# Seven block products in place of eight in the up-projections of two of the three feed-forward groups

## Chip, cores and metric

One NeuronCore of a Trainium2 chip runs the whole kernel. The metric is the device time of one launch in microseconds. The kernel before takes 2788.84 us (median of 3 runs, 2787.46 to 2789.62).

## What is computed

A two-layer network runs over 640 tokens: 512 latent tokens and 128 context tokens, 1024 channels each. Each layer is feed-forward, token mixing (attention and a Fourier branch), feed-forward, each with a modulation in front and a normalisation behind. The change touches only the two feed-forward sub-layers of each layer, so four in all:

```python
def _swiglu(u, w_up, w_down):            # w_up: 1024 x 5632, w_down: 2816 x 1024
    a, g = jnp.split(u @ w_up, 2, axis=-1)
    return (jax.nn.silu(g) * a) @ w_down
```

`a` is the value and `g` the gate. Everything is float32.

## The kernel before

**Layout.** Channels lie on the 128 partitions, tokens along the free dimension. The 1024 input channels are 8 blocks `k` of 128. The 640 tokens are 2 halves `h` of HT = 320. The 2816 hidden channels are 22 blocks, done in three groups of 8, 8 and 6 (`GROUPS`).

**Precision.** Each float32 operand is split in two parts of fewer bits, high and low: `Uh`/`Ul` for the modulated input, `w_hi`/`w_lo` for a weight, `Hh`/`Hl` for the hidden values. One block product is three matmuls into one accumulator: high by high, high by low, low by high.

**Weights.** They come as a stream of tiles of 16 blocks of 128x128 (1 MB). SP loads tile t into `w_raw[t % 2]` when the tile two before it has been split (`s_wsplit`). ACT rounds it to `w_hi` (`round_tile`, L922), DVE subtracts for `w_lo` (`low_tile`, L1240). Both are one tile ahead of TensorE. An up tile holds, for one hidden block, 8 blocks of the value and 8 of the gate.

**Up stage** (`ffn`, loops `up` on TensorE, ACT and DVE). For one tile TensorE does, for each token half, 8 block products into the value bank and 8 into the gate bank of one PSUM "use" (2 banks; four uses go round): 2 x 16 x 3 = 96 matmuls of 320 columns (L631, L633, L634). Then ACT takes silu of the gate bank into `sg` (`gate_half`, L1009), DVE multiplies with the value bank into `hf` (`product`, L1424), rounds to `Hh` (L1433) and subtracts for `Hl` (L1434). Every second tile DVE also works off two chunks of the conditioning weights (`ada_pair`, L1260 and L1262, four passes over 1024 columns), which ACT loads (`load_ada`).

**Down stage.** After each group four weight tiles (three after the group of 6) bring the hidden blocks back to 1024 channels (L444 to L447; `down_halves`, L489 to L493, after the last group), and DVE adds the result into `X`. The down stage starts on the first hidden blocks at once and waits for the last one block by block (`hidden_ready`).

**First group.** Its first 4 tiles (`EARLY`) are handled apart (`opening`, `first_up`), with the buffers `spare_f` and `spare_h`. The remaining 4 go through the loop `up`.

**POOL** does nothing but four constants at the start. `link` on DVE is a wait for DVE's own last instruction.

Of the kernel before, what the change touches and what calls it, by code (L numbers as in the profile page):

```python
# [13 lines left out]
P = 128  # L14
# [33 lines left out]
PIECES = 11  # L48
BIAS_STEP = {1: 0, 2: 1, 3: 2, 5: 3, 6: 4, 7: 5}
# [46 lines left out]
def build(nc, a):  # L96
    ctx = ExitStack()
    with ctx:
# [7 lines left out]
        X = sb("X", [P, KD, T])  # L106
        Uh = sb("Uh", [P, KD, T], F32R)
        Ul = sb("Ul", [P, KD, T], F32R)
        w_raw = sb("w_raw", [P, 2, 16, P])
# [42 lines left out]
        spare_f = spare("spare_f", 5120, 13312)  # L152
        spare_h = spare("spare_h", 61440, 81920)
# [132 lines left out]
        s_out = sem("y_stored")  # L286

# [11 lines left out]
        s_stands = {e: sem("wait_taken_" + e) for e in ("pe", "act", "dve")}  # L299
        block = ctx.enter_context(nc.Block())  # L300

        def make(which, **other):
# [6 lines left out]
                kv=s_kv, ada=s_adone, dve=s_dve, wraw=s_wload[0], whi=s_whi)  # L309
            first = dict(use=4, tile=1, ada=1, u=2 * KD, u32=2 * KD, mrg=4) | other  # L310
# [63 lines left out]
        def _(pe):  # L374

            C = make("tile use full h u mean sum sqsum var att sc max exp pt ptc o of fill fev mix mrg".split(), u=0)
# [236 lines left out]

            def ffn(pending):
# [4 lines left out]
                for group, size in enumerate(GROUPS):  # L619
# [17 lines left out]
                    pairs(size // 2 - (EARLY // 2 if group == 0 else 0), 2, 4, up)  # L637
# [264 lines left out]
        def _(act):  # L902
            C = make("use full func mods u32 u xc sq added var std xn y att max exp pt ptc o mrg ada kv wraw whi".split())
# [19 lines left out]

            def down_tiles(with_ada):
                def trip(i):
                    round_tile()
                    if with_ada:
                        ada_pair()
                    round_tile()
                over(act, 2, [(C["wraw"], 16), (C["whi"], 2)] + [(C["ada"], 2)] * with_ada, trip, act_met)  # L930
# [4 lines left out]
            def ada_pair():  # L935


                for s in (1, 0):
                    c = C["ada"].at()
                    if not isinstance(c, int):  # L940
                        c = act.snap(c)
                    act.wait_ge(s_adone, c)
                    load_ada(c + FIRST_ADA, s)
                    C["ada"].next()
# [39 lines left out]
            def last_products(l, s, spares, more):  # L984

                round_tile()
                for i, spare in enumerate(spares):
                    round_tile(1 + i, spare)
# [90 lines left out]
            def ffn(l, s):  # L1079
# [4 lines left out]
                for group, size in enumerate(GROUPS):  # L1084
                    def up(i):
                        for e in range(4):
# [3 lines left out]
                            if e == 0:  # L1090
                                ada_pair()

                    start = use_no[0]
                    n = size // 2 - (EARLY // 2 if group == 0 else 0)
                    over(act, n, [(use, 4), (C["full"], 4), (C["func"], 4), (C["ada"], 2), (C["wraw"], 16),
                                  (C["whi"], 2)], up, act_met)
                    use_no[0] = start + 4 * n
# [125 lines left out]
        def _(dve):  # L1223
            C = make("use full func h mods u32 u mean sum sq sqsum added std xc xn att kv max sc exp of fill fev pt o mix mrg ada dve whi".split())
# [5 lines left out]
            def low_tile(spare=None):  # L1230
# [9 lines left out]
                dve.tensor_tensor(lo, w_raw[:, r, :, :], hi.bitcast(F32), ALU.subtract).then_inc(s_wsplit, 1)  # L1240

# [152 lines left out]
            def down(m, n_of, count, ada):  # L1394

                for n in range(count):
                    if n % 2 == 0:
                        low_tile()
# [13 lines left out]
            def down_loop(m, ada=None):  # L1412
                start = use_no[0]
                over(dve, 2, [(use, 4), (C["full"], 4), (C["whi"], 2)]
                     + ([(C["ada"], 2), (C["dve"], 3)] if ada else []),
                     lambda i: down(m, lambda n: i * 4 + n, 4, (lambda: ada(i)) if ada else None), dve_met)
                use_no[0] = start + KD
# [482 lines left out]
```

## Time and profile before

| | |
|---|---|
| median of 3 runs | 2788.84 us |
| the profiled execution, device time | 2792.42 us |
| its span, first to last instruction | 2790.6 us |
| TensorE busy in the span | 2731.4 us (98%) |
| DVE, ACT, POOL busy | 60%, 27%, 0% |
| mean granted TensorE clock | 0.993 of full |

Matmuls are pipelined: a row's duration is the time through the array, and the rate is seen from start to start. On DVE an instruction without a wait starts some 0.08 us before the one ahead of it ends, so there too the spacing counts.

### The profile page before, as it was taken

To read this page: it belongs to the slowest core of one execution; us is meant where nothing else is said; L and a number is where in the kernel's file an instruction comes from. 1 tells how busy PE (TensorE), PEld (TensorE's weight loads), DVE (VectorE), ACT (ScalarE), POOL (GpSimd) and SP (SyncE) were. 2 spreads that over 40 slices of the span, in tenths; PEclk is the share of its full clock that TensorE was granted. 3 is DMA by queue.
4 is the path that set the end of the run, shared out by engine and by line. 5 is a ranking of instruction groups with operands and counts; after the bars stand their busy time and mean duration, and the time that the engine had idled before them with its cause. 6 is when DMAs were issued, how large, how long until landed. Compare 5 with 4: busy or idle time off the path is not lost.

```text
span 2790.6 us, 47327 instructions
## 1 busy us (share of the span) xinstructions
PE 2731.4 (98%) x18772; PEld 2702.6 (97%) x18772; DVE 1664.6 (60%) x3108; ACT 751.4 (27%) x1082; POOL 0.2 (0%) x4
## 2 busy tenths in 40 slices
PE   8999999899999999999999999998999999999997
PEld 8999999899999999999999999998999999999996
DVE  6645465765765864445686454676476568445456
ACT  4111112533221611111252111234242234111113
POOL 0000000000000000000000000000000000000000
PEclk9999999999999999999999999999999999999998
DMA  7434332211333132323223333322213322223231
GB/s 280 141 119 132 112 128 91 87 66 59 106 121 121 61 136 89 107 91 121 76 99 129 105 120 113 128 76 72 78 62 121 135 89 99 99 98 113 85 127 38
DMA packets 77781, 295.15 MB, mean 106 GB/s; under 512 B 25168, under 2 KB 31568, under 8 KB 54096
## 3 DMA queue, kind: packets, MB, share of 16 engines
q1 hardware_dynamic: 51552, 211.16, 21.8%
q10 hardware_dynamic: 26096, 82.16, 8.8%
q8 instruction: 91, 1.49, 0.2%
q14 instruction: 42, 0.34, 0.0%
HBM read 289.62 MB, written 6.82 MB: 106 GB/s over the span
## 4 chain that ended last, share of the span: by engine, by line
PE 92%; DVE 5%; DMA 1%; ACT 1%; issue 0%; ACTq 0%; SPq 0%; DVEq 0%
PE psum L633 12%; PE psum L634 12%; PE psum L631 12%; PE psum L446 6%; PE psum L444 6%; PE psum L447 6%; PE psum L489 3%; PE psum L492 3%; PE psum L493 3%; PE psum L858 3%; PE psum L860 3%; PE psum L861 3%; PE psum L693 2%; PE psum L876 1%; PE psum L874 1%; PE psum L877 1%
## 5 line engine op out<-in xcount | busy, mean ns | idle before, releaser
L631 PE MATMUL psum<-Uh,w_hi 128*128 128x320 f32 x2304 | 712.0, 309 | 0.0
L633 PE MATMUL psum<-Ul,w_hi 128*128 128x320 f32 x2304 | 711.9, 309 | 0.0
L634 PE MATMUL psum<-Uh,w_lo 128*128 128x320 f32 x2304 | 711.9, 309 | 0.0
L922 ACT ACTIVATE w_hi<-w_raw 128x2048 fp32r<-128x2048 f32 x166 | 317.6, 1913 | 590.5 <-PE psum L444 317.2
L631 PEld LDWEIGHTS psum<-Uh,w_hi 128*128 128x128 f32 x2304 | 432.5, 188 | 0.2 <-issue 0.2
L633 PEld LDWEIGHTS psum<-Ul,w_hi 128*128 128x128 f32 x2304 | 432.5, 188 | 0.0
L634 PEld LDWEIGHTS psum<-Uh,w_lo 128*128 128x128 f32 x2304 | 432.5, 188 | 0.0
L1240 DVE TENSOR_TENSOR w_lo<-w_raw,w_hi 128x2048 fp32r<-128x2048 f32 x166 | 380.3, 2291 | 81.1 <-ACT w_hi L922 76.7
L1424 DVE TENSOR_TENSOR hf<-sg,psum 128x320 f32<-128x320 f32 x176 | 85.7, 487 | 409.5 <-ACT sg L1009 407.6
L447 PE MATMUL psum<-Hh,w_lo 128*128 128x320 f32 x1024 | 316.2, 309 | 0.0
L444 PE MATMUL psum<-Hh,w_hi 128*128 128x320 f32 x1024 | 316.2, 309 | 0.0
L446 PE MATMUL psum<-Hl,w_hi 128*128 128x320 f32 x1024 | 316.2, 309 | 0.0
L1009 ACT ACTIVATE sg<-psum 128x320 f32<-128x320 f32 x176 | 77.0, 437 | 866.6 <-PE psum L634 614.8
L1408 DVE SCALAR_TENSOR_TENSOR X<-psum,mods,X 128x320 f32 (+2 forms) x192 | 72.6, 434 | 237.0 <-PE psum L447 237.0
L1260 DVE CUSTOM_DVE_ANT_0 junk<-ada_w,csilu 128x1024 bf16<-128x1024 f32 x144 | 176.0, 1222 | 62.8 <-DVEq L1724 48.4
L447 PEld LDWEIGHTS psum<-Hh,w_lo 128*128 128x128 f32 x1024 | 192.5, 188 | 0.0
L444 PEld LDWEIGHTS psum<-Hh,w_hi 128*128 128x128 f32 x1024 | 192.5, 188 | 0.0
L446 PEld LDWEIGHTS psum<-Hl,w_hi 128*128 128x128 f32 x1024 | 192.5, 188 | 0.0
L1262 DVE CUSTOM_DVE_ANT_0 junk<-ada_w,csilu 128x1024 bf16<-128x1024 f32 x144 | 176.4, 1225 | 5.0
L858 PE MATMUL psum<-Uh,w_hi 128*128 128x320 f32 x512 | 158.4, 309 | 0.9 <-DVE Ol L1651 0.9
L860 PE MATMUL psum<-Ul,w_hi 128*128 128x320 f32 x512 | 158.2, 309 | 0.0
L861 PE MATMUL psum<-Uh,w_lo 128*128 128x320 f32 x512 | 158.2, 309 | 0.0
(236 smaller groups left out, 4903.0 us busy)
## 6 DMA issues: line engine op xcount, KB each, us to landing
w_raw<-in_wstream SPq DMA_DIRECT2D x184, 1024.0 KB, 4.9
ada_w<-in_ada ACTq DMA_DIRECT2D x145, 512.0 KB, 3.7
first_w<-in_ada SPq DMA_DIRECT2D x9, 512.0 KB, 14.3
first_w<-in_ada_first SPq DMA_DIRECT2D x6, 512.0 KB, 9.1
gath<-in_rpb SPq DMA_DIRECT2D x128, 24.0 KB, 3.4
G<-gath ACTq DMA_DIRECT2D x4, 768.0 KB, 4.5
X<-in_xT SPq DMA_DIRECT2D x8, 320.0 KB, 15.1
yT<-X SPq DMA_DIRECT2D x16, 160.0 KB, 1.8
```

Source lines behind the costliest of these rows:

```text
L444: m1 = pe.matmul(out, wh, rh, start=(k == 0), stop=False)
L446: pe.matmul(out, wh, rl, start=False, stop=False)
L447: mm = pe.matmul(out, wl, rh, start=False, stop=(k == nk - 1))
L631: m1 = pe.matmul(out, wh, rh, start=(k == 0), stop=False)
L633: pe.matmul(out, wh, rl, start=False, stop=False)
L634: mm = pe.matmul(out, wl, rh, start=False, stop=(k == KD - 1))
L858: m1 = pe.matmul(out, wh, rh, start=(k == 0), stop=False)
L860: pe.matmul(out, wh, rl, start=False, stop=False)
L861: mm = pe.matmul(out, wl, rh, start=False, stop=(k == KD - 1))
L922: act.activation(hi, w_raw[:, r, :, :], ACT.Copy).then_inc(s_whi, 1)
L1240: dve.tensor_tensor(lo, w_raw[:, r, :, :], hi.bitcast(F32), ALU.subtract).then_inc(s_wsplit, 1)
L1262: i = dve.tensor_tensor_reduce(junk[:, :], ada_w[:, s, :], csilu[:, 1, :], 1.0, 0.0, ALU.mult, ALU.add, acc4[:, 1, s:s + 1])
```

## The change

In groups 2 and 3 of each feed-forward sub-layer (8 + 6 = 14 tiles, four times, 56 tiles) an up tile is taken as a 2x2 block matrix: value and gate by the two halves of the input channels (4 blocks each). The input is a 2x2 block matrix too: two halves of the input channels by two token halves. The 2x2 product is made from seven block products (Winograd's form of Strassen's scheme) instead of eight. Each product is 4 blocks deep, 4 x 3 = 12 matmuls of 320 columns.

- **Operands of the weights**: parts 0, 1 and 3 and four sums. POOL makes the sums, 4 instructions of 512 columns per tile (`weight_sums`), into columns of `Uh` and `Ul` that no product reads. ACT rounds and DVE splits each of the 7 operands by itself, 512 columns each (`round_operand`, `low_operand`), into a ring in `w_hi`/`w_lo`. Operand j of the next tile takes the place of operand j of this one, after product j.
- **Operands of the tokens**: four sums for each of 4 block rows, made once per sub-layer by POOL (`token_sums`, 4 x 10 instructions of 320 columns) during the loop tiles of the first group. ACT rounds and DVE splits them into `Th`/`Tl`.
- **Products**: three accumulators x, y, z in PSUM. ACT copies them out while they grow (`copy_product`, four copies of 320 columns per tile into `snaps`). DVE makes the two value halves by two additions (`hf`), POOL adds the late gate (`late_gate`), ACT takes silu of `snaps[3]` and of x.
- **Hidden values** (`hidden_half`): `Hh` and `hf` are both products with `sg`, the latter in place, and `Hl` their difference; the cast is gone.
- The loading of conditioning chunks is spread over two tiles (`ada_chunk`). The loops of the first group and of the down stage on ACT and DVE are written out.
- After the last group ACT waits until the last use is free before it writes `spare_f`, whose place `snaps` and `Th` share.

```diff
+OPERANDS = (("part", 0), ("sum", 0), ("sum", 1), ("part", 1), ("sum", 2), ("sum", 3), ("part", 3))
...
+            def seven_products(i):                                    # TensorE
...
+                U = (Uh, Ul)
+                for _ in range(2):
+                    u, v = next_use(), next_use()
+                    x, y, z = bank(u, 0, 0, HT), bank(u, 1, 0, HT), bank(v, 0, 0, HT)
+                    order = ((x, moving(U, 0, 0), True, 0), (y, summed(0), True, 0), (x, summed(1), False, 1),
+                             (z, moving(U, 4, 0), True, 0), (x, summed(2), False, 3), (y, moving(U, 4, 1), False, 2),
+                             (x, summed(3), False, 4))
+                    for j, (out, mv, start, copied) in enumerate(order):
+                        if copied:
+                            pe.wait_ge(s_snap, C["snap"].at(-copied))
+                        if j < 6:
+                            pe.wait_ge(s_opsplit, C["opsplit"].next())
...
+                        for k in range(4):
...
+                        mm.then_inc(s_prod, 1)
...
+            def seven_products(prepare, s):                           # ACT
...
+                product_done()
+                act.wait_ge(s_add, C["add"].at(1))
+                copy_product(0, x)
+                prepare(0)
+                product_done()
+                copy_product(1, y)
+                prepare(1)
+                product_done()
+                act.wait_ge(s_add, C["add"].at())
+                copy_product(2, x)
+                prepare(2)
+                product_done()
+                prepare(3)
+                product_done()
+                act.wait_ge(s_func, C["func"].at())
+                copy_product(3, x)
+                prepare(4)
...
+                product_done()
+                prepare(5)
+                act.wait_ge(s_late, C["late"].next())
+                act.wait_ge(s_free, use.at())
+                act.activation(sg[:, 1, :], snaps[:, 3, :], ACT.Silu).then_inc(s_func, 1)
...
+                product_done()
+                act.activation(sg[:, 0, :], x, ACT.Silu).then_inc(s_func, 1)
...
+                prepare(6)
...
+            def seven_products(at, prepare, between=None):            # DVE
...
+                for j in range(4):
+                    prepare(j)
...
+                mark(dve.tensor_tensor(hf[:, 0, :], snaps[:, 0, :], z, ALU.add), "add")
+                if between is not None:
+                    between()
+                for j in range(4, 6):
+                    prepare(j)
...
+                mark(dve.tensor_tensor(hf[:, 1, :], snaps[:, 2, :], y, ALU.add), "add")
+                dve.wait_ge(s_add, C["add"].at())
+                hidden_half(at, 1)
+                hidden_half(at, 0)
+                prepare(6)
...
+            def weight_sums(r):                                       # POOL
...
+                n1 = step(pool.tensor_tensor(part_sum(0), part(r, 2), part(r, 3), ALU.add), "wsum")
+                pool.wait_ge(s_wsum, n1)
+                n2 = step(pool.tensor_tensor(part_sum(1), part_sum(0), part(r, 0), ALU.subtract), "wsum")
+                step(pool.tensor_tensor(part_sum(2), part(r, 0), part(r, 2), ALU.subtract), "wsum")
+                pool.wait_ge(s_wsum, n2)
+                step(pool.tensor_tensor(part_sum(3), part(r, 1), part_sum(1), ALU.subtract), "wsum")
...
+                def trip(i):
+                    weight_sums(r ^ 1)
+                    late_gate()
+                    weight_sums(r)
+                    late_gate()
```

## Rows read from the trace of the kernel before

**Rows 1.** The page: busy time and share of each engine, then the slices.

```profile
PE 2731.4 (98%) x18772; PEld 2702.6 (97%) x18772; DVE 1664.6 (60%) x3108; ACT 751.4 (27%) x1082; POOL 0.2 (0%) x4
...
PE   8999999899999999999999999998999999999997
...
DVE  6645465765765864445686454676476568445456
```

**Rows 2.** Windows: first sub-layer's loop tiles of group 1, groups 2 and 3.

```profile
core 0: us, PE busy (x) PEld busy (x) DVE busy (x) ACT busy (x) POOL busy (x), PEclk, DMA share, GB/s
...
89.50:146.00 56.50, 56.50 (x385) 56.25 (x384) 38.61 (x62) 10.95 (x12) 0.00 (x0) 1.00 0.46 144
...
202.40:315.20 112.80, 112.80 (x771) 112.80 (x770) 59.13 (x92) 21.38 (x23) 0.00 (x0) 1.00 0.37 120
...
371.40:455.80 84.40, 84.40 (x578) 84.40 (x577) 49.14 (x78) 15.98 (x17) 0.00 (x0) 1.00 0.34 118
```

**Rows 3.** Groups by line, TensorE, and one line's own view (duration min/median/max).

```profile
L633 PE MATMUL psum<-Ul,w_hi 128*128 128x320 f32 x2304 | 711.9, 309 | 0.0
...
L631 PE MATMUL psum<-Uh,w_hi x2304: 307/309/408, 89.6 to 2723.7; 128*128 128x320 f32 x192
```

**Rows 4.** Timeline of ACT in group 2: start us, us, instruction, idle before it.

```profile
216.84 0.44 ACT L1009 ACTIVATE sg<-psum 128x320 f32<-128x320 f32 x1 [6.60 <-DVE acc L1262]
...
223.88 0.44 ACT L1009 ACTIVATE sg<-psum 128x320 f32<-128x320 f32 x1 [4.79 <-PE psum L634]
230.92 0.44 ACT L1009 ACTIVATE sg<-psum 128x320 f32<-128x320 f32 x1 [6.60 <-PE psum L634]
```

**Rows 5.** Waits over the whole run: us in total, times, longest.

```profile
ACT sg L1009 <- PE psum L634: 614.8, 119, 6.7
DVE hf L1424 <- ACT sg L1009: 407.6, 139, 5.7
...
PE psum L462 <- DVE sqtotal L1339: 12.5, 4, 6.6
```

**Rows 6.** Timeline of DVE in group 2 and group 3, with a conditioning pair.

```profile
210.27 0.49 DVE L1424 TENSOR_TENSOR hf<-sg,psum 128x320 f32<-128x320 f32 x1 [3.20 <-ACT sg L1009]
210.91 0.33 DVE L1433 CAST Hh<-hf 128x320 f32 x1
211.36 0.49 DVE L1434 TENSOR_TENSOR Hl<-hf,Hh 128x320 f32 x1
211.77 1.22 DVE L1260 CUSTOM_DVE_ANT_0 junk<-ada_w,csilu 128x1024 bf16<-128x1024 f32 x1
...
217.31 0.49 DVE L1424 TENSOR_TENSOR hf<-sg,psum 128x320 f32<-128x320 f32 x1 [0.19 <-ACT sg L1009]
...
378.56 2.29 DVE L1240 TENSOR_TENSOR w_lo<-w_raw,w_hi 128x2048 fp32r<-128x2048 f32 x1 [0.33 <-DVE mods L1267]
380.77 0.48 DVE L1424 TENSOR_TENSOR hf<-sg,psum 128x320 f32<-128x320 f32 x1
```

**Rows 7.** Groups by line and shape, DVE and ACT: busy us, mean ns.

```profile
L1240 DVE TENSOR_TENSOR w_lo<-w_raw,w_hi 128x2048 fp32r<-128x2048 f32 x166 | 380.3, 2291 | 81.1 <-ACT w_hi L922 76.7 <-DVE mods L1267 2.2 <-DVE mods L1275 1.3
...
L1434 DVE TENSOR_TENSOR Hl<-hf,Hh 128x320 f32 x144 | 71.0, 493 | 18.3 <-DVE Hh L1433 0.9
...
L1354 DVE RECIPROCAL std<-std 128x320 f32<-128x320 f32 x12 | 25.8, 2153 | 15.5 <-ACT std L957 15.5
```

```profile
L922 ACT ACTIVATE w_hi<-w_raw 128x2048 fp32r<-128x2048 f32 x166 | 317.6, 1913 | 590.5 <-PE psum L444 317.2 <-DVE acc L1262 84.4 <-PE psum L858 74.0
...
L1046 ACT ACTIVATE Uh<-u 128x320 fp32r<-128x320 f32 x16 | 7.5, 471 | 0.5
```

**Rows 8.** Groups by line, POOL: one of its four rows, all alike.

```profile
L1896 POOL MEMSET const-bfloat16-1.0<- 128x1 bf16 x1 | 0.1, 102 | 0.0
```

**Rows 9.** Timeline of DVE at the last group's end, in the last sub-layer.

```profile
2724.86 0.49 DVE L1424 TENSOR_TENSOR hf<-sg,psum 128x320 f32<-128x320 f32 x1 [5.45 <-ACT sg L1009]
...
2725.93 0.49 DVE L1434 TENSOR_TENSOR Hl<-hf,Hh 128x320 f32 x1
```

**Rows 10.** DMA issues: KB each, us from issue to landing.

```profile
w_raw<-in_wstream SPq DMA_DIRECT2D x184, 1024.0 KB, 4.9
```

More of the change, by code:

```diff
@@ L374, in _ @@
         def _(pe):
-            C = make("tile use full h u mean sum sqsum var att sc max exp pt ptc o of fill fev mix mrg".split(), u=0)
+            C = make("tile use full h u mean sum sqsum var att sc max exp pt ptc o of fill fev mix mrg opsplit prod snap tlow".split(), u=0)
             tile, use = C["tile"], C["use"]
@@ L635, in up @@
                                 filled(mm)
-                    pairs(size // 2 - (EARLY // 2 if group == 0 else 0), 2, 4, up)
+                    if group == 0:
+                        pairs((size - EARLY) // 2, 2, 4, up)
+                    else:
+                        if group == 1:
+                            pe.wait_ge(s_tlow, C["tlow"].next(4))
+                        start = use_no[0]
+                        over(pe, size // 2, [(tile, 2), (use, 4), (C["prod"], 14), (C["opsplit"], 12), (C["snap"], 8)],
+                             seven_products, pe_met)
+                        use_no[0] = start + 2 * size
                     made = C["h"].at()
@@ L902, in _ @@
         def _(act):
-            C = make("use full func mods u32 u xc sq added var std xn y att max exp pt ptc o mrg ada kv wraw whi".split())
+            C = make("use full func mods u32 u xc sq added var std xn y att max exp pt ptc o mrg ada kv wraw whi wsum prod snap late add tsum".split())
             use = C["use"]
@@ L924, in down_tiles, with round_token_sums @@
+            def round_token_sums(k):
+                act.wait_ge(s_tsum, C["tsum"].next(10))
+                act.activation(Th[:, :, k, :], snaps[:, :, :], ACT.Copy).then_inc(s_thi, 1)
             def down_tiles(with_ada):
-                def trip(i):
+                for i in range(2):
                     round_tile()
@@ L986, in last_products @@
                 round_tile()
+                act.wait_ge(s_free, use.at())
                 for i, spare in enumerate(spares):
@@ L1091, in up @@
                                 ada_pair()
[L1093 to L1097, printed above, removed]
+                            if e % 2 == 1:
+                                round_token_sums(2 * i + e // 2)
+                    if group == 0:
+                        for i in range((size - EARLY) // 2):
+                            up(i)
+                    else:
+                        seven_run(size)
                     if group < 2:
@@ L1412, in down_loop @@
             def down_loop(m, ada=None):
[L1413 to L1417, printed above, removed]
+                for i in range(2):
+                    down(m, lambda n: i * 4 + n, 4, (lambda: ada(i)) if ada else None,
+                         (low_tile, low_tile if i == 0 else first_operands))
             def product():
@@ L1557, in up @@
                             for h in range(2):
-                                evacuate(bass.ds(i * 2 + (m + done), 1), h)
+                                evacuate(i * 2 + (m + done), h)
                                 if (m, h) == (0, 0):
                                     more_chunks(i)
-                    start = use_no[0]
-                    n = (size - done) // 2
-                    over(dve, n, [(use, 4), (C["full"], 4), (C["func"], 4), (C["h"], 4), (C["ada"], 2),
-                                  (C["dve"], 4 + 3), (C["whi"], 2)], up, dve_met)
-                    use_no[0] = start + 4 * n
+                            split_token_sums(2 * i + m)
+                    if group == 0:
+                        for i in range((size - done) // 2):
+                            up(i)
+                    else:
+                        seven_run(size, more_chunks)
                     chunk += size - done
```

256 lines of the change are left out of this document (240 added, 16 removed).

## The prediction

> **What bounds the kernel now.** I read the page's busy line first [rows 1]: TensorE is busy 98% of the span, DVE 60%, ACT 27%, POOL 0%. The slices say that this holds from end to end. The windows [rows 2] narrow it to the stages that change: in groups 2 and 3 TensorE has no idle time at all, at a full granted clock (2.4 GHz), while DVE works 59.1 of 112.8 us and ACT 21.4. The waits agree [rows 5]: ACT waits for TensorE (614.8 us) and DVE for ACT (407.6 us), and the longest total wait of TensorE is 12.5 us, at a normalisation. So in these stages time is the number of matmuls times their spacing. The duration of 309 ns [rows 3] isn't the spacing. It is seen from the gates [rows 4]: one comes every 7.04 us (216.84, 223.88, 230.92), and between two of them are 48 matmuls, so 0.1467 us each. A tile of 96 takes 14.08 us, and 112.8 us hold 8 of them.
>
> **What is removed.** A tile goes from 96 matmuls to 7 x 12 = 84, same shape. That is 12 x 0.1467 = 1.76 us less per tile, which then takes 12.32 us. With 56 tiles: 98.6 us. Each product lasts 1.76 us, and everything below has to be measured against that, not against 3.7 us, which the durations would suggest.
>
> **TensorE's new waits.** At each product it now waits for an operand and often for a copy of its accumulator. The present loop has waits and a branch at each use boundary, and the spacing of 7.04 us shows no cost. The worst L631 is 0.1 us over the median [rows 3]; at each of 392 product boundaries that would be 39 us. I take 0 and keep 39 as the other end. A copy has one product (1.76 us) to be made: 0.44 us [rows 4] plus some 0.3 us of latency. It fits, if ACT is at hand.
>
> **ACT.** From 1913 ns for 2048 columns and 471 for 320 [rows 7], 512 columns cost 0.63 us. Per tile: 7 x 0.63 + 4 copies x 0.44 + 2 silus x 0.45 = 7.1 us of 12.32. It fits. ACT is in order though: behind its wait for the late gate (POOL) and for sums (POOL) stand the copies that TensorE waits for.
>
> **DVE.** From 2291 ns for 2048 columns and 493 for 320 [rows 7], 512 columns cost 0.69 us, or 0.61 from start to start, since a following instruction starts 0.08 us early (378.56 to 380.77 is 2.21 us for one of 2.29 [rows 6]). A linked one of 320 columns takes 0.63 to 0.64 from start to start, an unlinked one 0.41 (210.27, 210.91, 211.36, 211.77 [rows 6]). A conditioning pair takes 5.5 us (211.77 to 217.31). For two tiles:
> 14 low parts x 0.61 = 8.5; 4 additions, half of them linked, 2.1; hidden halves 4 x (0.63 + 0.63 + 0.41) = 6.7; one pair 5.5. The sum is 22.8 us of 24.64, or 93%.
> DVE goes from idle to nearly full. The order has to be gone through as well. Product 3 of a tile ends 7.04 us into it, ACT's rounding makes it 7.9, and DVE has low part 3 done at 8.5. In a tile with a pair there follow the addition (8.9), the pair (14.4), low parts 4 and 5 (15.6), the second addition (16.2), both hidden halves (19.6) and low part 6 (20.2). TensorE needs those three at 19.4, 21.1 and 22.9. The next tile catches up, since it has no pair: its hidden halves end at about 28.3, and low part 3 is again ready 8.5 us into the tile after. So TensorE isn't held. If instead each low part takes its full 0.69 us and a wait of 0.15 us (what a link adds), two tiles take 26.0 us, 0.7 us per tile too much: 39 us. I take 0, since operands lie ready when DVE comes to them.
>
> **POOL.** No row has arithmetic on POOL; its rows are four constants [rows 8]. Call p the time of its sum of 512 columns. From below p = 0.69 us, DVE's own price. From above I take the slowest elementwise row, the reciprocal of 320 columns in 2153 ns [rows 7]: 6.7 ns a column, p = 3.4. A simple addition is nearer to the first: I take 1.5 times DVE's price, p = 1.04, and 0.74 for 320 columns. A tile has four sums and a late gate, 4.9 us of 12.32. They may start when low part 5 is split (3.3 us into a tile without a pair) and when the raw tile has landed; its slot is free at about 3 us of the tile before, and landing takes 4.9 us [rows 10]. ACT wants the first sum at 4 us of that tile. It comes at 4.5, and the copy behind it is needed only at 7.04. It fits up to p of about 2. The Trainium skill ("GPSIMD Engine Reference", section 3.1) gives 4497 ns for 2048 columns of such an addition; an estimate from that page is 1.1 us for 512, and by it the sum below doesn't change. No run here shows it yet.
>
> **Token sums.** 40 POOL instructions x 0.74 = 30 us per sub-layer lie beside the 56 us of the first group's loop tiles. ACT gets 4 x 1.3 us and DVE 4 x 1.4 us more there, where DVE is busy 38.6 of 56.5 us [rows 2]. TensorE needs the result one down stage (56 us) later. Cost 0.
>
> **Starts of the down stage.** Now the last hidden block is ready about 1.6 us after its gate (2724.86 to 2726.42 [rows 9]); then 0.63 + 0.63 + 0.49 = 1.75 us. TensorE's cover there is 5 blocks x 3 x 0.147 = 2.2 us in group 3, about used up already. I count 0.3 us x 4 = 1.2 us. In group 2 the cover is three times as long. The weights' first operands of a group are made in the down stage, in the time of the tile that they replace, and operands 4 to 6 have four products' time. ACT's new wait for the last use stands ahead of a buffer needed some 28 us later: 0.
>
> **Sum.** The profiled execution took 2792.4 us. 2792.4 - 98.6 + 1.2 = 2695.0. It lay 3.6 us above the median, so I forecast 2691.4, say 2692 us.
>
> **Rivals.**
> (A) Forecast: TensorE stays the bound, 2686 to 2705.
> (B) DVE or the new waits show through. DVE has 7% left, and the two ends above are 39 us each. The price of one is 2692 + 39 = 2731; the case holds 2705 to 2783. Part-way contention with POOL falls here too. For it speaks that each tile with a pair already runs 1.8 us late and only the next one repairs it.
> (C) DVE and POOL exclude each other. Nearly all new DVE work reads two operands in SBUF, and so does POOL. If such instructions can't run at the same time, two tiles need the sum of both. DVE's are 14 x 0.69 + 12 x 0.49 + 4 x 1.22 = 20.4 us; POOL's are 8p + 2 x 0.71p = 9.4p. TensorE is held once 20.4 + 9.4p exceeds 24.64 (p over 0.45, so at any p within the bounds), and the kernel is slower than before once it exceeds 28.16: p over 0.82 us. At p = 1.04 it is 30.2 us, 1.0 us per tile more than before: 2789 + 57 = 2846. At p = 0.69 it is 2754. Nothing in the trace speaks for or against it, because POOL never works beside DVE; if it is so, the 40% that DVE is idle is no room for POOL.
> The Trainium skill ("SBUF — State Buffer", section "Who interferes with whom") states it: a DVE instruction with two SBUF inputs and a GpSimd instruction that reads SBUF contend for one read port, and the second to issue is blocked until the first ends. With that page's rule and the other page's 1.1 us the estimate would be 2869. No row here shows the pair of them.
> (D) POOL itself is too slow. At p = 3.4 a tile needs 4 x 3.4 + 2.2 = 15.8 us on POOL, 1.7 more than before: 2789 + 97 = 2886. It begins to cost at p over 2 and is slower than before from p of about 3.1.
> (E) The scheme doesn't shorten TensorE, for instance because accumulating again into a bank costs time. The counts in the code are plain: 84 matmuls of an unchanged shape.
>
> **How the numbers follow.** A 0.42, B 0.16, C 0.34, D 0.06, E 0.02. In C p below 0.82 leaves it faster, which takes 0.03 of its chance, and some 0.03 lie within 0.2%. Faster by over 0.2% is then 0.59, within it 0.04, slower 0.37; 0.2% (5.6 us) is about what a measurement of this kernel can tell from no change. The range must take in C: it runs from 2686 to 2875, which leaves out the slow end of C and most of D, some 0.14. A's own range is 2686 to 2705. It is wide because faster and slower cases both are likely.
>
> **What would show it.** Under A: TensorE without idle time in the windows of groups 2 and 3, 12.3 us from tile to tile, DVE above 90% busy there with low parts near 0.69 us, POOL's sums near 1.04 us. Under B: the same durations, but TensorE waiting for low parts or copies. Under C: durations of DVE or POOL that grow where both are active (low parts well over 0.69 us, conditioning passes over 1.22 us), 15 us per tile and TensorE idle, perhaps with a clock below full after it. Under D: sums of over 2 us with DVE's durations unchanged, ACT waiting for POOL. I'm wrong in the working if DVE's durations are unchanged and the time is still above 2735.

## The result and the profile after

The changed kernel takes 2863.82 us (median of 4 runs, 2862.61 to 2865.26) beside 2789.23 us for the kernel before on the same chip: a ratio of 1.027, 95% interval 1.025 to 1.0285. It is slower by 75 us where the forecast was 2692. Its profiled execution took 2865.26 us, with a span of 2863.4. Of the rivals it is C, the exclusion of DVE and POOL, that fits, though not by its own figures. Three steps of the sum failed with it (POOL's fit, the start of group 3, the token sums), one of them in a place where POOL isn't involved.

The page of the changed kernel first: busy time and count of each engine, then the slices of the span.

```profile
PE 2688.3 (94%) x18100; PEld 2640.2 (92%) x18100; DVE 2116.7 (74%) x3572; ACT 980.7 (34%) x1658; POOL 603.1 (21%) x444
...
PE   8999998899999999898999989898999999998996
...
DVE  7769778855765885968887796986476578679497
...
POOL 0534232000000062413106340400000002533130
```

Against [rows 1] TensorE has 672 matmuls fewer (56 tiles x 12), and its busy time fell by only 43 us, not by 98.6. DVE went from 60% to 74%, and POOL has 603 us of work where it had none. Seven slices of TensorE fell from 9 to 8, and POOL works in six of them.

Windows of the changed kernel, by stage, in the first sub-layer: loop tiles of the first group up to the down stage, down stage, group 2, group 3. Columns as in [rows 2].

```profile
88.20:152.80 64.60, 59.52 (x386) 58.74 (x384) 54.03 (x63) 14.63 (x16) 46.17 (x32) 0.95 0.35 107
152.80:209.30 56.50, 56.46 (x385) 56.46 (x386) 33.47 (x56) 9.11 (x8) 15.34 (x13) 1.00 0.40 126
209.30:326.50 117.20, 104.85 (x674) 102.77 (x673) 111.31 (x149) 51.59 (x101) 50.30 (x36) 0.96 0.35 111
...
382.90:474.80 91.90, 79.84 (x507) 77.78 (x505) 86.23 (x119) 38.69 (x75) 36.52 (x26) 0.94 0.29 99
```

| stage, us | before | after | times |
|---|---|---|---|
| first group's loop tiles | 56.6, later 56.3 | 64.6, later 59.2 | 1 and 3 |
| group 2 | 112.6 | 117.1 to 117.3 | 4 |
| group 3 | 84.5 | 91.6 to 91.9 | 4 |
| down stages of the first group | 56.3 | 56.4, 56.4, 58.0, 59.2 | 4 |
| first 162 matmuls of the last down stage, to the next one's start | 32.8 | 34.2 | 4 |

The times run from the first matmul of a stage to the first of the next. Groups 2 and 3 lose about 4 x (4.5 + 7.3) = 47 us, the first groups 8.0 + 3 x 2.9 = 17, the down stages of the first group 5 and the last ones 6: 75 in all. Against the forecast, which wanted 12.32 us a tile (4 x 172.5 = 690 us for groups 2 and 3), the 4 x (117.2 + 91.9) = 836 us are 146 too many.

In group 2 DVE is busy 111.3 of 117.2 us (95%, against 59.1 of 112.8 in [rows 2]). TensorE is idle 12.4 us of it and busy 104.9, though 672 matmuls at 0.1467 us are 98.6: the other 6 us are matmuls at the lower clock, which the granted clock of 0.96 shows.

Waits of the changed kernel over the whole run (total us, times, longest):

```profile
PE psum L682 <- ACT snaps L1040: 53.3, 28, 3.9
PE psum L682 <- DVE w_lo L1446: 41.3, 31, 2.3
...
ACT w_hi L1025 <- POOL sums L2082: 81.3, 39, 4.8
...
ACT Th L1107 <- POOL snaps L2060: 99.0, 13, 10.7
```

TensorE now waits for copies (L1040) and low parts (L1446), where the longest total of [rows 5] was 12.5 us. ACT waits for POOL's sums. That these stand behind both is seen in e2 below: with the sums cut short, 15.5 of the 94.6 us are left.

### The profile page after: what moved, and what is told of

Read it like the earlier page. It is cut to its first block and busy times, and to the rows that moved or that the text cites. A ratio compares the mean times of both kernels' runs of the same rounds, so it can differ in the third digit from the quotient of the medians.

```text
span 2863.4 us, 48177 instructions
## 1 busy us (share of the span) xinstructions
PE 2688.3 (94%) x18100; PEld 2640.2 (92%) x18100; DVE 2116.7 (74%) x3572; ACT 980.7 (34%) x1658; POOL 603.1 (21%) x444
## 5 line engine op out<-in xcount | busy, mean ns | idle before, releaser
L682 PE MATMUL psum<-Th,w_hi 128*128 128x320 f32 x896 | 292.9, 327 | 94.9 <-ACT snaps L1040 53.3
L1433 DVE TENSOR_TENSOR w_lo<-w_raw,w_hi 128x2048 fp32r<-128x2048 f32 x110 | 263.5, 2396 | 73.5 <-ACT w_hi L1009 72.9
L687 PE MATMUL psum<-Th,w_lo 128*128 128x320 f32 x896 | 286.7, 320 | 0.0
L686 PE MATMUL psum<-Tl,w_hi 128*128 128x320 f32 x896 | 286.4, 320 | 0.0
L682 PEld LDWEIGHTS psum<-Th,w_hi 128*128 128x128 f32 x896 | 175.5, 196 | 111.1 <-DVE w_lo L1446 66.1
L2082 POOL TENSOR_TENSOR sums<-w_raw 128x512 f32<-128x512 f32 x56 | 79.3, 1415 | 724.4 <-DVE w_lo L1446 411.0
L1025 ACT ACTIVATE w_hi<-sums 128x512 fp32r<-128x512 f32 x224 | 139.0, 627 | 248.5 <-POOL sums L2082 81.3
L682 PE MATMUL psum<-Uh,w_hi 128*128 128x320 f32 x672 | 211.9, 315 | 0.0
L686 PE MATMUL psum<-Ul,w_hi 128*128 128x320 f32 x672 | 210.7, 313 | 0.0
L687 PE MATMUL psum<-Uh,w_lo 128*128 128x320 f32 x672 | 209.6, 312 | 0.0
L687 PEld LDWEIGHTS psum<-Th,w_lo 128*128 128x128 f32 x896 | 177.2, 198 | 0.0
```

Source lines behind the costliest of these rows:

```text
L682: m1 = pe.matmul(out, hi[:, k, :], rh, start=(start and k == 0), stop=False, skip_group_check=not start)
L686: pe.matmul(out, hi[:, k, :], rl, start=False, stop=False, skip_group_check=not start)
L687: mm = pe.matmul(out, lo[:, k, :], rh, start=False, stop=(k == 3), skip_group_check=not start)
L1025: act.activation(two_rows(operand(w_hi, j, w_slot[0])), operand_source(op_raw[0], j), ACT.Copy)\
```

## Why DVE and POOL don't run side by side

Timeline of DVE in group 2 of the changed kernel (start us, duration, instruction, idle before it in brackets), and of POOL in the same stretch:

```profile
239.76 0.49 DVE L1658 TENSOR_TENSOR Hh<-sg,hf 128x320 f32 x1 [0.27 <-DVE hf L1685]
240.29 1.47 DVE L1659 TENSOR_TENSOR hf<-sg,hf 128x320 f32<-128x320 f32 x1
241.88 1.38 DVE L1667 TENSOR_TENSOR Hl<-hf,Hh 128x320 f32 x1
243.18 1.58 DVE L1658 TENSOR_TENSOR Hh<-sg,hf 128x320 f32 x1
```

```profile
240.11 1.29 POOL L2082 TENSOR_TENSOR sums<-w_raw 128x512 f32<-128x512 f32 x1 [6.59 <-DMA w_raw<-in_wstream]
241.48 1.43 POOL L2084 TENSOR_TENSOR sums<-sums,w_raw 128x512 f32<-128x512 f32 x1
242.87 1.54 POOL L2085 TENSOR_TENSOR sums<-w_raw 128x512 f32<-128x512 f32 x1
```

The first DVE instruction has no POOL beside it until its last 0.14 us and takes 0.49 us, as [rows 7] have it. The next starts at 240.29, while POOL's first sum is under way (240.11 to 241.40), and ends at 241.76, 0.36 us after that sum: alone it takes 0.49, so it can have done little before. POOL's next sum then outlasts it in turn. The two take turns, and each duration holds the wait for the other. One instruction of each together takes 1.50 us (the next two of DVE end at 243.26 and 244.76). The groups by line show DVE's products of 320 columns at nearly twice their 493 ns:

```profile
L1659 DVE TENSOR_TENSOR hf<-sg,hf 128x320 f32<-128x320 f32 x112 | 107.3, 958 | 7.8
...
L2082 POOL TENSOR_TENSOR sums<-w_raw 128x512 f32<-128x512 f32 x56 | 79.3, 1415 | 724.4 <-DVE w_lo L1446 411.0 <-DMA w_raw<-in_wstream 259.3 <-issue 54.0
```

The shortest instance of L2082 is 1.26 us: that is POOL's own price for 512 columns. How a sum that comes late reaches TensorE is seen in a tile with a conditioning pair. Four rows of the timeline, from POOL, ACT (two) and TensorE:

```profile
257.74 1.26 POOL L2082 TENSOR_TENSOR sums<-w_raw 128x512 f32<-128x512 f32 x1 [8.31 <-DVE w_lo L1446]
...
259.04 0.63 ACT L1025 ACTIVATE w_hi<-sums 128x512 fp32r<-128x512 f32 x1 [4.04 <-POOL sums L2082]
259.57 0.42 ACT L1040 ACTIVATE snaps<-psum 128x320 f32<-128x320 f32 x1
...
260.12 0.41 PE L682 MATMUL psum<-Th,w_hi 128*128 128x320 f32 x1 [2.08 <-ACT snaps L1040]
```

DVE had the pair to do and split low part 5 late, POOL may not write its sums before that, ACT stands at the rounding of the first sum, and the copy that TensorE needs is the next instruction in ACT's queue. TensorE loses 2.08 us, though the product that the copy reads had ended at 256.3.

## The experiments

Each edit is against the changed kernel unless it says otherwise. "Before" is the kernel before, run beside it.

**e2: POOL's four sums and the late gate of 8 columns.** Products read raw parts in place of the sums.

```diff
-n1 = step(pool.tensor_tensor(part_sum(0), part(r, 2), part(r, 3), ALU.add), "wsum")
+n1 = step(pool.tensor_tensor(short(part_sum(0)), short(part(r, 2)), short(part(r, 3)), ALU.add), "wsum")
```

> The changed kernel, but POOL's four weight sums and its late gate are cut to 8 columns each (same instructions, same waits, same order); ACT and DVE take the raw parts where they took the sums, so the up-projections of groups 2 and 3 are not those of the reference. DVE's, ACT's and TensorE's work is unchanged. Theory L (DVE and POOL exclude each other while both read SBUF): with POOL's reads gone the seven-product stages are bound by TensorE at 12.3 us per tile, DVE's low parts and hidden multiplies are back at 0.68 and 0.49 us; 98.6 us less than the kernel before, plus about 20 us still lost in the first groups, where POOL still makes the token sums: about 2712 us. Theory F (DVE is simply too full, or TensorE's new waits cost time, POOL's work is harmless): DVE has as much to do as in the changed kernel, so the time stays between 2840 and 2865 us.

Measured: 2740.34 us, ratio to before 0.982 (0.9806 to 0.9839). That is 123 us less than the changed kernel, with every instruction still issued. Group by line and windows (group 2; group 3 and 0.9 us of the stage behind it) of e2:

```profile
L1662 DVE TENSOR_TENSOR hf<-sg,hf 128x320 f32<-128x320 f32 x112 | 55.2, 493 | 7.7
```

```profile
209.30:307.80 98.50, 98.50 (x675) 98.50 (x673) 82.67 (x151) 50.62 (x100) 15.47 (x36) 1.00 0.42 137
...
364.10:444.60 80.50, 76.61 (x513) 76.35 (x512) 67.52 (x122) 38.51 (x76) 12.35 (x26) 0.98 0.37 124
```

DVE's product is back at 493 ns, and group 2 runs at exactly the 12.3 us a tile of the forecast, TensorE without idle time. Counts, waits and copies are those of the changed kernel, so TensorE's new waits cost nothing, as forecast. What is lost in group 2 comes from POOL's full-width sums; whether it is their reading beside DVE or only the time that they take is told apart by e5 and e8. But group 3 still takes 79.5 to 80.6 us, not 73.9, and that was expected by neither theory. TensorE and ACT at its start in e2:

```profile
368.33 1.67 ACT L1028 ACTIVATE w_hi<-w_raw 128x512 fp32r<-128x512 f32 x3 [15.75 <-DVE acc L1482]
371.12 0.44 ACT L1043 ACTIVATE snaps<-psum 128x320 f32<-128x320 f32 x1 [1.12 <-DVE acc L1482]
371.68 0.41 PE L685 MATMUL psum<-Th,w_hi 128*128 128x320 f32 x1 [3.89 <-ACT snaps L1043]
```

ACT waits 15.75 us for DVE's passes of a conditioning pair (`acc`), which stands between the last down tile and group 3, then again for its last pass, 1.12 us ahead of the copy. TensorE stands 3.89 us.

**e7: e2 with that extra pair ahead of the last down use.**

```diff
-                    if group == 1:
-                        chunks(chunk)(0)
-                        chunk += 2
+                        down_loop(mods[s], chunks(chunk) if s == 0 else None,
+                                  [lambda: chunks(extra)(0)] if group == 1 else ())
```

> The run with POOL's weight sums and late gate cut to 8 columns (raw parts taken as operands, so groups 2 and 3 are not the reference's), and one thing more: the conditioning pair that DVE works off between the last down product and the first low parts of group 3 now runs before DVE takes the last down use. Theory S (the start of group 3): in that run ACT stood 15.8 us in its wait for that pair, so operands 4 to 6 and the first copy came late, TensorE idled 3.9 us at product 2 and then ran at half clock; without it group 3 takes 6 x 12.3 us as it should, 5 to 7 us less in each of four sub-layers: about 2717 us. Rival: the first copy is late for another reason (ACT's order alone), and the time stays at 2740 us.

Measured: 2711.94 us, ratio 0.9725 (0.971 to 0.974), 28.4 us less than e2, 7.1 per sub-layer. Group 2 stays at 98.5 us; the window of group 3:

```profile
364.40:438.30 73.90, 73.90 (x507) 73.90 (x505) 61.54 (x112) 37.75 (x74) 11.49 (x26) 1.00 0.37 124
```

Both groups are now as forecast: 4 x (98.5 + 73.9) = 690 us. What e7 is above 2692, 20 us, lies elsewhere: 17 us of it in the first groups, beside the token sums.

**e3: the sums and the late gate on DVE, full width.** DVE gets four sums of 512 columns and one addition of 320 more per tile.

```diff
+                n1 = step(dve.tensor_tensor(part_sum(0), part(r, 2), part(r, 3), ALU.add))
...
+                mark(dve.tensor_tensor(snaps[:, 3, :], snaps[:, 3, :], snaps[:, 1, :], ALU.add), "late")
```

> The changed kernel with POOL's four weight sums and the late gate done by DVE, same values, same places; POOL keeps only the token sums. DVE, already the fuller engine, gets 8 x 0.60 + 2 x 0.41 us and two waits more for two tiles, some 6.4 us. Theory L: the sum for two tiles is then 22.8 + 6.4 = 29.2 us on DVE alone, 14.6 us per tile against 14.9 with POOL, and 14.08 in the kernel before; with 20 us lost in the first groups: about 2835 us, that is FASTER than the changed kernel although its busiest helper got more work. Theory F: 3.2 us per tile more than the changed kernel's 14.9: about 3040 us.

Measured: 2843.85 us, ratio 1.0196 (1.018 to 1.021), 20 us less than the changed kernel though DVE, the fuller engine, has all of POOL's weight sums and late gates. Without an exclusion I had expected 3040. Groups by line, and the window of the first group 2, of e3:

```profile
L1678 DVE TENSOR_TENSOR hf<-sg,hf 128x320 f32<-128x320 f32 x112 | 55.1, 492 | 8.3 <-DVE Hh L1677 0.7
```

```profile
210.60:326.70 116.10, 105.63 (x674) 104.85 (x673) 102.64 (x186) 49.78 (x99) 0.00 (x0) 0.93 0.36 113
```

POOL is still, DVE's durations are clean, and the four groups 2 take 116.1, 112.8, 112.8 and 116.1 us, where they took 117 with POOL's help. 186 DVE instructions do what DVE's 149 and POOL's 36 did.

**e5: conditioning passes of groups 2 and 3 cut from 1024 to 16 columns** (POOL as in the changed kernel).

```diff
-                    more_chunks = chunks(chunk)
+                    more_chunks = chunks(chunk, 16 if group else D)
```

> The changed kernel, with the conditioning passes of DVE in groups 2 and 3 cut from 1024 to 16 columns (14 x 4 passes per sub-layer; those modulation values are then wrong). DVE loses 4.6 us for two tiles. POOL is as it was. Theory L: what two tiles need from DVE's two-input instructions and POOL together is 15.5 + 11.8 = 27.3 us, 13.7 us per tile, still above TensorE's 12.3: about 2789 - 24 + 20 = 2785 us, and DVE's multiplies stay well over 0.49 us. Theory F: DVE has 17.5 us of work for 24.64 us of TensorE and is out of the way: about 2712 us.

Measured: 2766.54 us, ratio 0.992 (0.990 to 0.994), between the two expectations and nearer to that of the exclusion. Group 2 and the product's group by line:

```profile
209.30:312.70 103.40, 99.65 (x675) 98.60 (x674) 95.44 (x150) 51.47 (x100) 51.37 (x36) 1.00 0.41 130
```

```profile
L1659 DVE TENSOR_TENSOR hf<-sg,hf 128x320 f32<-128x320 f32 x112 | 108.3, 967 | 7.8
```

The product still takes 967 ns: POOL is in its way as before. What is gone is DVE's own work (28 passes per sub-layer; my expectation had counted 56), and the tile goes from 14.65 to 12.9 us. So POOL's sums at their full length, with all that waits for them, nearly fit once DVE has less to do. The sum by spacings for two tiles, 8.4 + 4.9 + POOL's 11.8 = 25.1 (worked out below), stands against 25.8 measured. I had expected 27.3, having counted durations where spacings hold.

**e4: the kernel before, with POOL working on data of its own** in layer 0: 74 additions from the start of group 2, 90 memsets in group 3, 74 copies in group 2 of the second feed-forward sub-layer. Apart from waits of ACT and DVE for the end of POOL's stretches, nothing else of the kernel changes.

```diff
+phase(14, 74, lambda o: pool.tensor_tensor(o, csilu[:, 0, 0:512], csilu[:, 1, 0:512], ALU.add))
+phase(26, 90, lambda o: pool.memset(o, 0.0))
+phase(TILES - 33 + 14, 74, lambda o: pool.tensor_copy(o, csilu[:, 0, 0:512]))
```

> The kernel before, with POOL working beside it on data of its own that nobody waits for, in layer 0: 74 additions of 512 columns with two SBUF inputs during group 2 of the first sub-layer, 90 memsets of 512 columns (it writes, reads nothing) during group 3, 74 copies of 512 columns (one input) during group 2 of the second feed-forward sub-layer. Theory L: in the first stretch DVE's instructions with two SBUF inputs (low parts 2.29 us, conditioning passes 1.22, Hl 0.49) take up to one POOL addition (about 1.3 us) longer, and POOL's additions take up to one DVE instruction longer, while the multiply that reads PSUM and one SBUF input stays at 0.49; with memsets nothing gets longer; with copies it is as with additions but shorter. The cast (one input, 0.33 us) shows which interface matters. TensorE has the slack, so the time stays within 0.3% of 2789 us. Theory F: no DVE duration changes in any stretch.

Measured: 2824.25 us, ratio 1.013 (1.011 to 1.014); the time was to be within 0.3%. DVE's groups by line and shape in group 2 of e4, with POOL adding all the while:

```profile
L1246 DVE TENSOR_TENSOR w_lo<-w_raw,w_hi 128x2048 fp32r<-128x2048 f32 x8 | 26.6, 3319 | 0.7 <-ACT w_hi L926 0.7
...
L1442 DVE TENSOR_TENSOR Hl<-hf,Hh 128x320 f32 x15 | 20.7, 1383 | 1.8
...
L1266 DVE CUSTOM_DVE_ANT_0 junk<-ada_w,csilu 128x1024 bf16<-128x1024 f32 x8 | 18.1, 2258 | 0.1
L1441 DVE CAST Hh<-hf 128x320 f32 x15 | 11.1, 738 | 2.2 <-DVE hf L1432 0.7
...
L1432 DVE TENSOR_TENSOR hf<-sg,psum 128x320 f32<-128x320 f32 x15 | 7.2, 480 | 3.1 <-ACT sg L1015 2.6
```

```profile
202.50:315.00 112.50, 112.50 (x770) 112.50 (x769) 103.78 (x89) 21.30 (x25) 112.50 (x61) 1.00 0.35 115
```

This is the disputed cost by itself. Against [rows 6, 7] every DVE instruction with two SBUF inputs grows by 0.9 to 1.0 us, most of one POOL addition (1.29): 2.29 to 3.32 us, 0.49 to 1.38, 1.22 to 2.26. The cast grows too (0.33 to 0.74). The product that takes one input from PSUM stays at 0.48. Beside POOL's copies, in the third stretch, it was the same in small: 2.29 to 2.63, 1.22 to 1.57, 0.49 to 0.69, the PSUM product at 0.49. TensorE loses nothing here: DVE's 103.8 us still fit into 112.5, which is why a kernel with a DVE 60% busy could hide it.

The 34.5 us came from the stretch with memsets (group 3: 117.6 us for 84.5). DVE's timeline in group 3 of e4, and what TensorE waited for:

```profile
372.51 1.23 DVE L1268 CUSTOM_DVE_ANT_0 junk<-ada_w,csilu 128x1024 bf16<-128x1024 f32 x1
...
376.31 35.95 DVE L1273 COPY mods<-acc 128x4 f32<-128x4 f32 x1
```

```profile
PE psum L635 <- DVE w_lo L1246: 31.1, 1, 31.1
```

Beside memsets the two-input pass is unchanged (1.23 us), but a copy of 4 columns stood 36 us.

**e10: memsets back to back in group 2, then with a gap after each in group 3** (e4's kernel).

```diff
+            phase(14, 60, lambda o: pool.memset(o, 0.0), 3)
+            phase(26, 60, lambda o: pool.memset(o, 0.0), 0)
```

> The kernel before with POOL on data of its own, in layer 0: 60 memsets of 512 columns back to back (up to four under way) in group 2 of the first sub-layer; 60 memsets of which each waits for the one before it, in group 3; 60 copies, each waiting for the one before, in group 2 of the second feed-forward sub-layer. Theory W (a DVE instruction of a mode that needs the shared interface for its writes is held until POOL lets go, and POOL's overlapping memsets never let go, as the small copy of 35.95 us in the first probe suggests): in the first stretch DVE's first cast or small copy hangs until the memsets are over, some 28 us, and TensorE may idle; in the second the memsets' gaps let it in, and casts and copies are longer by at most one memset (0.6 us), while instructions with two SBUF inputs stay at 2.29, 1.22 and 0.49 us in both. Rival: the 35.95 us had nothing to do with the memsets and no cast or copy takes more than 1 us.

Measured once: 2795.68 us. DVE's and POOL's timeline in group 2 of e10:

```profile
209.65 1.50 DVE L1441 CAST Hh<-hf 128x320 f32 x1
...
216.87 12.78 DVE L1273 COPY mods<-acc 128x4 f32 x1
```

```profile
201.68 27.95 POOL L1788 MEMSET probe<- 128x512 f32 x60 [201.22 <-PE psum L635]
```

The copy ended when the memsets did (229.6 us). The cast had come through after 1.50 us, where I had expected it to stand to the end. With gaps, casts took 0.33 to 0.56 us and no copy over 0.61. So memsets without a gap can keep a cast or copy of DVE from starting, but not each time; what decides it is open.

**e8: POOL keeps the sums; all conditioning pairs of groups 2 and 3 are made in the down stages.**

```diff
+            def down_loop(m, pairs):
+                places = (1, 2, 3) if len(pairs) == 6 else (1, 3)
...
-                    seven_products(bass.ds(i * 2, 1), low_operand, lambda: more_chunks(i))
+                    seven_products(bass.ds(i * 2, 1), low_operand)
```

> The changed kernel with POOL's sums as they are, and all conditioning pairs of groups 2 and 3 moved into the two down stages ahead of them (6 pairs in each in the first sub-layer of a layer, 4 in each in the last); values as in the reference. Theory L: the seven-product stages then have what the run with short conditioning passes had, two tiles needing 27 us less what overlaps; that run took 2766.5 us, and with the start of group 3 mended some 20 us less: about 2747 us, still above 2717 because DVE and POOL exclude each other. If the down stages get too full for DVE (about 50 of 56 us in the first sub-layer of a layer), TensorE waits there and it is 2760 to 2780 us. Theory F (no exclusion): TensorE-bound, 2715 us.

Measured: 2740.15 us, ratio 0.982 (0.981 to 0.984). Windows of group 2, down stage and group 3 in the first sub-layer, and of group 2 in the second feed-forward sub-layer:

```profile
209.50:316.60 107.10, 102.27 (x674) 101.22 (x674) 98.38 (x129) 51.05 (x100) 51.76 (x36) 0.97 0.32 101
316.60:372.90 56.30, 56.30 (x386) 56.30 (x385) 51.02 (x84) 8.56 (x9) 7.05 (x4) 1.00 0.53 178
372.90:448.90 76.00, 74.61 (x505) 73.83 (x505) 68.07 (x89) 37.59 (x73) 38.44 (x26) 1.00 0.26 90
...
1099.30:1200.50 101.20, 99.33 (x674) 98.54 (x674) 93.23 (x114) 51.06 (x100) 51.48 (x36) 1.00 0.24 83
```

The down stage takes six pairs and stays full on TensorE, its DVE at 51.0 of 56.3 us. In the second feed-forward sub-layer of each layer, with four pairs, group 2 takes 101.2 and 100.8 us, 25.2 per two tiles: what the sum by spacings gives without the pair (25.1), and near the 24.64 of TensorE. POOL's weight sums last 1.4 to 1.7 us in the mean, no less than in the changed kernel (1.4 to 1.6). So it isn't their length alone that makes 117 us there, but their length beside a DVE that is full. In the first sub-layer of each layer the sixth pair runs into group 2, which takes 107.1 us.

**e6: e8 with sums and late gate on DVE, and the cast back in the hidden halves.**

```diff
-                link(dve.tensor_tensor(hh, sg[:, h, :], hf[:, h, :], ALU.mult))
+                link(dve.tensor_copy(hh, hf[:, h, :]))
```

> A version meant to beat both kernels: weight sums and late gate on DVE (POOL only makes the token sums), all conditioning pairs of groups 2 and 3 moved into the down stages, and the hidden halves with a cast again (one product in place, then a cast of 0.33 us, then the difference), which POOL can't hold up any more. DVE for two tiles: 22 x 0.60 + 0.4 + 2.1 + 0.8 + 4 x (0.63 + 0.45 + 0.41) = 22.5 us of 24.64. Theory L: bound by TensorE, 2789 - 98.6 + about 20 us lost in the first groups to the token sums: 2710 us, 2700 to 2725. Rival: DVE at 91% of its time plus waits in ACT's and DVE's fixed order hold TensorE up by 0.5 us per tile or more, with half clock behind it: 2740 to 2780 us.

Measured (median of 5 runs): 2726.37 us, ratio 0.977 (0.976 to 0.9785), just above my range of 2700 to 2725 and, with e9, the fastest version that computes everything. Group 2 of the first and of the second feed-forward sub-layer:

```profile
209.70:314.20 104.50, 101.44 (x674) 101.18 (x673) 87.71 (x165) 50.62 (x99) 0.00 (x0) 0.97 0.33 104
...
1096.20:1194.70 98.50, 98.50 (x675) 98.50 (x674) 81.17 (x150) 50.80 (x99) 0.00 (x0) 1.00 0.24 86
```

The second is as fast as a TensorE without waits can be, and 2.7 us faster than with POOL's sums (e8). In the first, the down stage ahead has six pairs, and DVE is still at the last of them (211.4 to 216.4) when group 2 has begun (209.7).

**e9: e6 with ACT's and DVE's part of the token sums one tile later**, so that ACT doesn't stand at a sum that isn't made.

```diff
-                            if e % 2 == 1:
-                                round_token_sums(2 * i + e // 2)
+                            if e % 2 == 1 and 2 * i + e // 2:
+                                round_token_sums(2 * i + e // 2 - 1)
```

> The version with sums on DVE and the pairs moved, and ACT and DVE take each of POOL's four token sums one tile later: the first three at the ends of loop tiles 2 to 4 of the first group, the fourth at the start of the down stage behind it. Theory T (the 20 us lost around the first group come from ACT and DVE standing in their fixed order in front of token sums that POOL hasn't finished): the loop tiles of the first sub-layer take 56 to 58 us in place of 62.8, the waits for the first down tile's low parts (9.3 us in four) go, about 10 us less than the 2726.4 of that version: 2716 us. Rival: the loss is contention between POOL's 160 sums and DVE in the first group, which is the same wherever they are taken up: 2726 us, or more if the fourth sum now crowds the down stage.

Measured: 2729.96 us, ratio 0.9785 (0.977 to 0.980), where I had expected 2716: no gain over e6. The loop tiles of the first groups went from 64.6 to 57.2 us, in the later sub-layers from 59.2 to 56.3, as expected. But the down stages behind them took 58.9 to 61.0 us (e6: 56.4 to 59.2), and groups 2 of the first sub-layers of a layer 107.2 and 107.5 (104.5 and 100.1). ACT at the last group of token sums in e9 (waits from 140 to 212 us):

```profile
ACT w_hi L1009 <- DVE acc L1496: 19.3, 2, 13.9
ACT Th L1103 <- POOL snaps L2088: 14.9, 2, 10.7
```

ACT still stands 10.7 us at one token sum. The wait had moved to another stage; it wasn't taken away.

## Why the prediction was wrong, step by step

- **Removed matmuls: right.** Groups 2 and 3 take 98.5 and 73.9 us in e7, 12.3 us a tile, as forecast.
- **TensorE's new waits: right at 0.** e2 and e7 have every wait and branch, and no idle time in group 2. The 39 us of the other end aren't there.
- **DVE's own sum, 93%: high, on the safe side.** In e7, where POOL hardly reads, DVE is busy 82.7 of 98.5 us in group 2 (84%, without the gaps that links leave). Its own work fits.
- **POOL's price p: mis-sized.** I took 1.04 us for 512 columns and 0.74 for 320; alone they take 1.26 to 1.29 and 0.87, so a tile asks 5.9 us of POOL and not 4.9. The Trainium skill's figure ("GPSIMD Engine Reference", section 3.1) had led to an estimate of 1.1 us, nearer but still short.
- **"It fits up to p of about 2": the step that failed.** I fitted POOL's 4.9 us into the 12.32 of a tile as if its time were its own. DVE's 93% was counted beside it, and the two had to be added. By the spacings of the rows, two tiles need 14 low parts x 0.60 = 8.4, 12 instructions of 320 columns x 0.41 = 4.9, 4 passes x 1.15 = 4.6 and POOL's 8 x 1.26 + 2 x 0.87 = 11.8: 29.7 us. Group 2 measures 2 x 14.65 = 29.3, where TensorE alone would need 24.6. The sum is an estimate, and its closeness is partly luck: one sum and one product in turn take 1.50 us, not 1.26 + 0.41, while DVE's instructions with a PSUM input aren't counted at all. e4 shows the exclusion itself. That it is the cause in this kernel follows from the others together: with DVE's work whole and POOL's cut (e2) the stage takes 98.5 us, with POOL's whole and DVE's cut (e5) 103.4, or moved away (e8, second sub-layers) 101, with both whole 117. The Trainium skill ("SBUF — State Buffer", section "Who interferes with whom") says so for two SBUF inputs against a GpSimd read. The traces agree: 2.29 us became 3.32 beside additions, and the pass beside memsets kept its 1.23.
- **The choice of A over C: wrong, for a weak reason.** I gave C less than A because "nothing in the trace speaks for or against it". The trace of the kernel before couldn't speak, but that is no evidence for A. By my own figures an exclusion costs time from p of 0.45 us on, no value within my bounds was below that, and with an exclusion and my own p of 1.04 the kernel had to be slower. So the sign hung on one unmeasured question, and I gave the answer that made it slower the smaller chance. The question can be put to the kernel before alone, as e4 does.
- **C's own time: close by offsetting errors.** It said 2846, measured is 2863.8. Its formula took durations (0.69 and 0.49 us) where starts come 0.60 and 0.41 apart; with the true p it gives 32.2 us for two tiles, 2.9 too many. And it left out the next items. (The 2869 beside it takes p = 1.13; with 1.1 as written the same formula gives 2861. It lies near the measured time by the same luck.)
- **Starts of the stages: wrong.** "Operands 4 to 6 have four products' time" looked at DVE's low parts alone and not at the pair queued ahead of them, on which ACT stands in order, with the copies behind it. In e2, without POOL's load, group 3 costs 5.5 to 6.7 us too much each time; e7 moved one pair and got 28.4 us back.
- **"0.3 us x 4" at the last down stage: too small.** TensorE waits 5.5 us there for the last hidden block (L530 <- Hl, 4 times), 3.0 in e7, where POOL hardly reads.
- **"Token sums. Cost 0": wrong, about 20 us.** POOL's additions of 320 columns alternate with DVE here as well, and their four groups add up to 53 us per sub-layer where I had 30. One of these groups, and a row of ACT's timeline, in the changed kernel:

```profile
L2060 POOL TENSOR_TENSOR snaps<-snaps,Ul 128x320 f32<-128x320 f32 x96 | 119.4, 1263 | 2.5
...
129.02 1.27 ACT L1107 ACTIVATE Th<-snaps 128x1280 fp32r<-128x1280 f32 x1 [10.72 <-POOL snaps L2060]
```

  ACT waited 10.72 us at the rounding of a token sum, and behind it stood the gates of the running tile. That the result was needed only 56 us later was true and beside the point: who waits for it is ACT's whole queue. e9 took ACT out of that wait, and the first groups' loops came back to 56.3 us, though the loss then turned up in the stages behind.
- **Signs named ahead.** Those of C came: low parts over 0.69 us (770 and 822 ns in the mean), 15 us a tile, TensorE idle, a clock below full. Under B durations would have been unchanged. But the median low part stayed at 0.68: 51 of 392 took over 0.75. The sign was clearer in the hidden halves, whose products had a median of 1.04 and 0.96 us.

What stays open: how much of the loss is idle time and how much the lower clock that follows it. In group 2 the window gives 12.4 and 6.2 us, but the ends of matmuls are modelled. And what the down stages' slack is worth beside token sums: e9's down stages overflow though DVE is busy 47 of 61 us in the first of them.

## What to carry to other kernels

Before work is put on an idle GpSimd, add its time to that of all VectorE instructions with two SBUF inputs, and ask whether the sum fits, since "40% idle" on VectorE is the only room that both have. Here a sum of 512 columns took 0.60 us of that room on VectorE and up to 1.26 on GpSimd, so that handing it over lost room: with the sums back on VectorE the kernel was 20 us faster (e3), and 14 us with the pairs moved (e6 against e8; e6 also has the cast back). Use the distance from start to start for such sums, not durations. And at each stage boundary follow the in-order queues by hand: a value that isn't needed for 50 us can still hold an engine whose next instruction is needed at once.

## What the runs showed of the hardware

- POOL's own prices alone: addition of 512 columns 1.26 to 1.29 us, 320 columns 0.87 us; memset of 512 columns 0.52 (e10) to 0.60 (e4) in the median, 0.47 from start to start in e4; copy 0.61.
- A short instruction can cost as much as what it meets: in e4 POOL's addition (1.29 us alone) takes up to 3.35 us, where it meets a DVE low part of 2.29. POOL in e4 (tile's view: min/median/max):

```profile
L1788 POOL TENSOR_TENSOR probe<-csilu x74: 1287/1549/3354, 201.2 to 338.4; 128x512 f32<-128x512 f32 x74
```

- Memsets of POOL leave DVE's two-input instructions alone, but held a DVE copy of 4 columns for 35.95 us (e4) and one for 12.78 us (e10); with a gap after each memset none took over 0.61 us. The Trainium skill ("SBUF — State Buffer", section "Who interferes with whom") has copy and cast among the instructions that can contend with GpSimd, where whichever comes first keeps the shared ports for the whole instruction. The traces agree that they are held, but these copies waited for many memsets of 0.5 to 0.6 us, not for one.
- Behind a wait of 2.30 us for a low part TensorE ran at the lower level (1.2 GHz) in group 2 of the changed kernel: matmuls 0.27 us apart instead of 0.147, for some 3.5 us from 235.14 on. Not every wait does this: behind the one of 2.08 us at 260.12 only the first matmul was slower (0.24 us), and the granted clock stayed at 1.00.
